# Expert gates of a two-block transformer layer: fp32r one-hot products of 256 columns, four tokens behind each of 64 score blocks

## What is computed

```
q = (xf @ wq).reshape(t, 8, 256)
v1, i1 = top_k(q[..., :128] @ keys1.T, 16);  v2, i2 = top_k(q[..., 128:] @ keys2.T, 16)
top_s, pos = top_k(v1[..., :, None] + v2[..., None, :], 16)      # over 16 x 16 candidates
expert = (i1 * 128 + i2)[pos]                                     # 8 x 16 = 128 picks a token
gate = softmax(top_s)
z = einsum('cd,ced->ce', x, u[expert]);  act = gelu(z) * gate
y = einsum('ce,ced->cd', act, v[expert])
```

## Time and profile before

| what | us |
|---|---|
| median of 3 runs (2815.0 to 2817.1) | 2816.63 |
| the profiled execution | 2815.1 |
| span of the profiled execution | 2813.3 |
| TensorE busy | 2759.1 (98%) |
| VectorE busy | 1811.2 (64%) |
| ScalarE busy | 1391.6 (49%) |
| GpSimd busy | 257.1 (9%) |

### The profile page before, as it was taken

The page is one execution under the profiler, slowest core; times in us unless marked ns, Lnnn a source line. Parts: engine busy times, 40 slices in busy tenths (PEclk is TensorE's granted clock), DMA queues, the critical chain, the costliest instruction groups (busy, mean ns, idle before and its releaser), DMA issues.

```text
span 2813.3 us, 49430 instructions
## 1 busy us (share of the span) xinstructions
PE 2759.1 (98%) x15452; PEld 2411.5 (86%) x15452; DVE 1811.2 (64%) x2894; ACT 1391.6 (49%) x2020; POOL 257.1 (9%) x342
## 2 busy tenths in 40 slices
PE   8999999899999999999999999999999999999998
PEld 6888877788888888889999999888888888888887
DVE  6666655657986666578886666666665555555555
ACT  5454545545565444455555554545554444444444
POOL 0000000000000000000004998000000000000000
PEclk9999999999999999999999999999999999999999
DMA  6544454464554444555565444666665556555574
GB/s 244 191 151 164 162 175 155 165 210 154 167 172 163 157 150 142 186 193 185 183 207 175 159 155 157 216 211 212 209 211 193 194 194 193 191 192 193 193 236 159
DMA packets 153551, 514.71 MB, mean 183 GB/s; under 512 B 17056, under 2 KB 33696, under 8 KB 152480
## 3 DMA queue, kind: packets, MB, share of 16 engines
q1 hardware_dynamic: 131904, 480.44, 52.0%
q10 hardware_dynamic: 21600, 33.70, 3.3%
HBM read 501.49 MB, written 12.58 MB: 183 GB/s over the span
## 4 chain that ended last, share of the span: by engine, by line
PE 59%; DVE 0%; ACT 0%; issue 0%; POOL 0%; DVEq 0%; ACTq 0%; POOLq 0%
PE bank L493 13%; PE bank L2111 8%; PE bank L2113 8%; PE bank L2112 8%; PE bank L498 6%; PE bank L478 3%; PE bank L479 3%; PE bank L480 3%; PE bank L2086 2%; PE bank L533 1%; PE bank L532 1%; PE bank L531 1%; PE bank L2061 0%; DVE act L1086 0%; PE bank L2131 0%
## 5 line engine op out<-in xcount | busy, mean ns | idle before, releaser
L455 DVE TENSOR_TENSOR w_lo<-raw,w_hi 128x1024 fp32r<-128x1024 f32 x904 | 1097.8, 1225 | 816.3 <-ACT w_hi L446 808.9
L446 ACT ACTIVATE w_hi<-raw 128x1024 fp32r<-128x1024 f32 x904 | 953.2, 1059 | 1027.5 <-PE bank L2113 369.3
L493 PE MATMUL bank<-act,w_hi 128*128 128x512 f32 x3072 | 787.9, 398 | 2.7 <-ACT w_hi L446 1.3
L493 PEld LDWEIGHTS bank<-act,w_hi 128*128 128x128 f32 x3072 | 554.1, 189 | 109.3 <-issue 6.2
L498 PEld LDWEIGHTS bank<-act,w_lo 128*128 128x128 f32 x3072 | 419.1, 190 | 31.2
L498 PE MATMUL bank<-act,w_lo 128*128 128x256 f32 x3072 | 428.1, 282 | 0.0
L2111 PE MATMUL bank<-w_hi,expert_act 128*128 128x512 f32 x1008 | 392.3, 389 | 0.1
L2112 PE MATMUL bank<-w_lo,expert_act 128*128 128x512 f32 x1008 | 392.2, 389 | 0.0
L2113 PE MATMUL bank<-w_hi,expert_act 128*128 128x512 f32 x1008 | 392.1, 389 | 0.0
L478 PE MATMUL bank<-act,w_hi 128*128 128x256 f32 x912 | 261.0, 286 | 3.3 <-DVE w_lo L455 2.7
L479 PE MATMUL bank<-act,w_hi 128*128 128x256 f32 x912 | 258.7, 284 | 0.0
(11 more groups left out here) (286 smaller groups left out, 2380.2 us busy)
## 6 DMA issues: line engine op xcount, KB each, us to landing
raw<-in_stream SPq DMA_DIRECT2D x904, 512.0 KB, 4.2
big<-in_ukv ACTq DMA_DIRECT2D x16, 512.0 KB, 5.2
z_kept<-cst ACTq DMA_DIRECT2D x64, 128.0 KB, 3.2
cst<-z_kept ACTq DMA_DIRECT2D x64, 128.0 KB, 3.9
big<-in_x SPq DMA_DIRECT2D x2, 1024.0 KB, 9.6
big<-in_rows ACTq DMA_DIRECT2D x2, 1024.0 KB, 8.8
big<-in_rg_w ACTq DMA_DIRECT2D x1, 2048.0 KB, 8.2
x_kept<-big ACTq DMA_DIRECT2D x1, 2048.0 KB, 6.6
```

Of the source, the lines that this page charges most:

```text
L446: act.activation(w_hi[:, s, :], raw[:, s, :], ACT.Copy).then_inc(hi_ready, 1)
L455: dve.tensor_tensor(w_lo[:, s, :], raw[:, s, :], w_hi[:, s, :].bitcast(F32), ALU.subtract).then_inc(lo_ready, 1)
L493: pe.matmul(bank[:, :], w_hi[:, s, kk * P:(kk + 1) * P], act2[:, k, :, :].rearrange("p a n -> p (a n)"), start=(k == 0), stop=False)
```

## The change

- `EARLY` becomes 96 and a new `LATE` is 32. `u_gates` now holds 64 score blocks, `u_late` 32. `z_kept` has 96 rows.
- Behind each score block of `u_gates`, after both units, come four tokens in place of eight split over the two units. Each engine's loop has 32 turns of two blocks.
- The gates are split once into `gate_hi` (fp32r, ScalarE) and `gate_lo` (the rest, VectorE). For one token, VectorE writes `weighted[:, s, :, :]`, 256 wide: the one-hot of the first index times the high gates, and beside it the same times the low gates, in one `scalar_tensor_tensor`. GpSimd's one-hot `hot[:, s, :]` is unchanged but for its type.
- The product of a token is one fp32r product with 256 columns. Two tokens fill a bank; a block uses two banks, `banks[0]`, `banks[1]` for even and `banks[4]`, `banks[5]` for odd blocks.
- ScalarE copies the low halves of a bank to `G` (two tokens, 256 values a partition), VectorE adds the high halves to `G` (`add_gates`).
- 64 of the 96 kept blocks are read back and multiplied in the first 32 turns of the stage `v` in place of `u_late`.

The other buffers only move (`hot`, `weighted`, `slot_t` and the parameters' tile `par`, which now also holds the second indices). The diff, cut to its core:

```diff
-         ("wqu", 4 * PH), ("u_decode", 2 * PH), ("u_gates", S // 8), ("u_late", NB // 2), ("v", NB)]
-EARLY = NB // 2
+         ("wqu", 4 * PH), ("u_decode", 2 * PH), ("u_gates", S // 4), ("u_late", NB // 4), ("v", NB)]
+EARLY = 3 * NB // 4
+LATE = NB - EARLY
...
# ScalarE, gate stage
+            act.activation(gate_hi.bitcast(F32R), gate_lo, ACT.Copy).then_inc(slots_kept, 1)
+
+            with act.Fori(0, S // 8) as i:
                 for n in range(2):
-                    def keep_gates(m):
-                        act.wait_ge(hot_used[3], i * 4 + 2 * n + m + 2)
-                        act.activation(G[:, :, bass.ds(i * 16 + (8 * n + 4 * m), 4)],
-                                       banks[m][:, :].rearrange("p (t b) -> p b t", t=4), ACT.Copy)\
-                           .then_inc(gate_kept[m], 1)
-                    ahead(split_hi, act, "u_gates", i, 2, n, units=(0,))
-                    keep_gates(0)
-                    ahead(split_hi, act, "u_gates", i, 2, n, units=(1,))
+                    for u in range(2):
+                        ahead(split_hi, act, "u_gates", i, 2, n, units=(u,))
                     act.wait_ge(unit_done, 2 * pair_of("u_gates", i, 2, n) + 2)
                     act.wait_ge(z_saved[n], i * 16 + (32 * PH + 1))
                     low_half(act, GZ[:, n, :], banks[2 + n])
-                    keep_gates(1)
+                    for half in range(2):
+                        act.wait_ge(hot_used[2 * half + 1], i * 2 + n + 2)
+                        act.activation(G[:, :, bass.ds(i * 8 + (4 * n + 2 * half), 2)],
+                                       GATE_BANKS[n][half].rearrange("p (t a b) -> p a b t", t=2, a=2)[:, 1, :, :],
+                                       ACT.Copy).then_inc(gate_low, 1)
                     wait_summed(act, block_of("u_gates", i, 2, n))
                     act.activation(GZ[:, n, :], GZ[:, n, :], ACT.Gelu).then_inc(gelu_ready[n], 1)
                     act.wait_ge(gelu_ready[n], i + (2 * PH + 2))
...
# ScalarE, stage v, first 32 turns
+            with act.Fori(0, (EARLY - LATE) // 2) as i:
+                for n in range(2):
+                    act.wait_ge(early_ready[n], i + (LATE // 2 + 1))
+                    act.dma_start(GB[:, n, :], z_kept[bass.ds(i * 2 + (LATE + n), 1), :, :]
+                                  .rearrange("o p n -> (o p) n")).then_inc(z_back[n], 16)
+                next_experts(i)
...
# VectorE, gate stage
+            def add_gates(i, n):
+                for half in range(2):
+                    dve.wait_ge(gate_low, i * 4 + (2 * n + half + 1))
+                    dest = G[:, :, bass.ds(i * 8 + (4 * n + 2 * half), 2)]
+                    high = GATE_BANKS[n][half].rearrange("p (t a b) -> p a b t", t=2, a=2)[:, 0, :, :]
+                    dve.tensor_tensor(dest, dest, high, ALU.add).then_inc(gate_kept[n], 1)
+
+            with dve.Fori(0, S // 8) as i:
                 for n in range(2):
-                    for s in range(8):
-                        tok = i * 16 + (8 * n + s)
-                        dve.wait_ge(hot_used[s % 4], i * 4 + (2 * n + s // 4) + 1)
-                        dve.tensor_scalar(hot[:, 0, s % 4, :], iota, slot_t[:, 0, bass.ds(tok, 1)],
-                                          slot_t[:, 2, bass.ds(tok, 1)], ALU.is_equal, ALU.mult).then_inc(hot1, 1)
-                        if s % 4 == 3:
-                            ahead(split_lo, dve, "u_gates", i, 2, n, units=(s // 4,))
+                    for s in range(4):
+                        tok = i * 8 + (4 * n + s)
+                        dve.wait_ge(hot_used[s], i * 2 + n + 1)
+                        dve.scalar_tensor_tensor(
+                            out=weighted[:, s, :, :], in0=iota.unsqueeze(1).broadcast_to([P, 2, P]),
+                            scalar=first_index[:, bass.ds(tok, 1)],
+                            in1=slot_t[:, 1:3, bass.ds(tok, 1)].broadcast_to([P, 2, P]),
+                            op0=ALU.is_equal, op1=ALU.mult).then_inc(hot1, 1)
+                        if s == 1 and n == 1:
+                            add_gates(i, 0)
+                        if s % 2:
+                            ahead(split_lo, dve, "u_gates", i, 2, n, units=(s // 2,))
                     add_halves(dve, GZ[:, n, :], banks[2 + n], block_of("u_gates", i, 2, n))
+                add_gates(i, 1)
...
# VectorE, stage v, first 32 turns
+                    next_expert(i, n)
+                    dve.wait_ge(z_back[n], i * 16 + (8 * LATE + 16))
+                    back = G[:, bass.ds(i * 2 + (LATE + n), 1), :].rearrange("p o n -> p (o n)")
+                    dve.tensor_tensor(back, GB[:, n, :], back, ALU.mult).then_inc(early_ready[n], 1)
...
# TensorE, gate stage
+            with pe.Fori(0, S // 8) as i:
                 for n in range(2):
                     pe.wait_ge(gelu_ready[n], i + (2 * PH + 1))
-                    for m in range(2):
-                        halves_out(pe, pair_of("u_gates", i, 2, n), n, banks[2 + n], units=(m,))
-                        pe.wait_ge(gate_kept[m], i * 2 + n + 1)
-                        for s in range(4):
-                            pe.wait_ge(hot1, i * 16 + (8 * n + 4 * m + s + 1))
-                            pe.wait_ge(hot2, i * 16 + (8 * n + 4 * m + s + 1) + 1)
-                            pe.matmul(banks[m][:, s * P:(s + 1) * P], hot[:, 1, s, :], hot[:, 0, s, :], start=True,
-                                      stop=True).then_inc(hot_used[s], 1)
+                    halves_out(pe, pair_of("u_gates", i, 2, n), n, banks[2 + n])
+                    pe.wait_ge(gate_kept[n], i * 2 + 1)
+                    for s in range(4):
+                        pe.wait_ge(hot1, i * 8 + (4 * n + s + 1))
+                        pe.wait_ge(hot2, i * 8 + (4 * n + s + 1) + 1)
+                        pe.matmul(GATE_BANKS[n][s // 2][:, (s % 2) * S:(s % 2 + 1) * S], hot[:, s, :],
+                                  weighted[:, s, :, :].rearrange("p a b -> p (a b)"), start=True, stop=True)\
+                          .then_inc(hot_used[s], 1)
```

More of the change, by code:

```diff
@@ L83 @@
 _n = 0
-for _name, _count in [("conv", 4 * CONV_J), ("rnn", 2 * KT), ("heads", 2 * H2), ("u_gates", S // 8),
-                      ("u_late", NB // 2)]:
+for _name, _count in [("conv", 4 * CONV_J), ("rnn", 2 * KT), ("heads", 2 * H2), ("u_gates", S // 4),
+                      ("u_late", LATE)]:
     HALVED[_name] = _n
@@ L157, in build @@
             pass
-        hot = sb("hot", [P, 2, 4, P])
+        weighted = sb("weighted", [P, 4, 2, P], F32R)
+        with nc.sbuf_tensor("below_hot", [P, CONST["causal"][0]], F32), \
+                nc.sbuf_tensor("hot", [P, 4, P], F32R) as hot:
+            pass
         cst = sb("cst", [P, CONST_W])
@@ L260, in build @@
         G = big[:, :].rearrange("p (b t) -> p b t", b=NB)
+        first_index = slot_t[:, 0, :]
+        second_index = par[:, 0:S]
+        gate_hi = slot_t[:, 1, :]
+        gate_lo = slot_t[:, 2, :]
+        GATE_BANKS = [[banks[0], banks[1]], [banks[4], banks[5]]]
         GZ = c("band").rearrange("p (s n) -> p s n", s=2)
@@ L615, in _ @@
                     pool.sem_inc(hot_turn, 1)
-                    pool.tensor_scalar(hot[:, 1, s % 4, :], iota, idx8[:, s:s + 1], None, ALU.is_equal)\
+                    pool.tensor_scalar(hot[:, s % 4, :], iota, idx8[:, s:s + 1], None, ALU.is_equal)\
                         .then_inc(hot2, 1)
@@ L1010, in expert_hi @@
                 act.activation(expert_hi_t[:, n, :], G[:, bass.ds(b, 1), :].rearrange("p o n -> p (o n)"), ACT.Copy)                   .then_inc(eh_ready, 1)
-            with act.Fori(0, EARLY // 2 - 1) as i:
+            with act.Fori(0, LATE // 2 - 1) as i:
                 late_turn(i)
@@ L1016, in _ @@
                 expert_hi(n, n, 2 * FIRST["u_late"])
-            late_turn(EARLY // 2 - 1)
+            late_turn(LATE // 2 - 1)
             for n in range(2):
-                act.wait_ge(act_ready[n], EARLY // 2 + 1)
-                act.wait_ge(early_ready[n], EARLY // 2 + 1)
+                act.wait_ge(act_ready[n], LATE // 2 + 1)
+                act.wait_ge(early_ready[n], LATE // 2 + 1)
             def next_experts(i):
@@ L1024, in next_experts @@
                     expert_hi(i * 2 + (2 + n), n, 2 * pair_of("v", i, 2, n) + 2)
-            with act.Fori(0, NB // 2 - 8) as i:
+            with act.Fori(0, (EARLY - LATE) // 2) as i:
[4 more added lines that the diff above has]
+                next_experts(i)
+            for n in range(2):
+                act.wait_ge(early_ready[n], EARLY // 2 + 1)
+            with act.Fori((EARLY - LATE) // 2, NB // 2 - 8) as i:
                 next_experts(i)
@@ L1682, in _ @@
                 ahead(split_lo, dve, "u_decode", 0, 2, _)
-            dve.wait_ge(slots_kept, 3)
-            with dve.Fori(0, S // 16) as i:
-                for n in range(2):
-                    for s in range(8):
-                        tok = i * 16 + (8 * n + s)
```

(44 more changed lines are left out.)

9 lines of the change are left out of this document (4 added, 5 removed).

## The result

The changed kernel takes 2830.89 us (median of 5 runs, 2830.15 to 2831.41), the kernel before 2816.28: the ratio is 1.0056, with a 95% interval of 1.0044 to 1.0067. It is 14.6 us slower. The forecast was 8.5 us slower, with a range of 2806 to 2836, in which 2830.9 lies. The profiled execution has a span of 2828.2 us, 14.9 more than before.

The account below looks back on a forecast made before the run. TensorE, busy 98%, was taken to wait on a chain through ScalarE and VectorE: 32 x 13.43 + 0.6 = 430.4, plus 178.8 for late scores, 609.2 us against 600.7, 8.5 us slower: 2823.6 us, range 2806 to 2836.

Parts of the forecast that it names:

- narrow bounds: Whole kernel: 2820 to 2832 us, the forecast case with the wide one-hot priced cheaper or dearer.
- price of the wide one-hot: VectorE, gate stage: 0.48 us long, 0.40 apart; bounds 0.34 apart, 3.5 us off, and 0.52 to 0.60, 7.7 more.
- What bounds, and the products: Gate stage: TensorE bounds; four products take 0.47 us in place of 0.93, a block 6.06 if nothing waits.
- rival A: Gate stage: faster, the chain does not reach TensorE, 6.06 us a block, 2781.6 us in all; chance 0.15.
- The chain: Gate stage: TensorE waits for tokens 2 and 3's one-hots behind VectorE's split, through ScalarE's DMA issue; 13.43 us per two blocks.
- The term that was too small: Chain's end, from ScalarE's high split to TensorE's next scores: 3.49 us, including 0.11 more for a product that waited.
- binding term: ScalarE's next split at 9.94 us after an odd block, with its loop jump, plus 3.49: 13.43 us per two blocks.
- The start: Gate stage's first block: tokens 2 and 3 come late, about 7.3 us, 0.6 more than the mean.
- B: Gate stage: about the same, only the short chain binds, 6.48 us a block, 2808.5 us in all; chance 0.15.
- C: Gate stage: slower, GpSimd governs, held up by wide one-hots, 7.0 us a block, 2842 us in all; chance 0.08.
- D: Gate stage: VectorE blocks behind GpSimd at unit 1's low split, 10 to 19 us more, about 2838; chance 0.05.
- What the profile was to show: Gate stage: two unequal blocks 13.4 us apart, and about 120 TensorE idle times or long weight loads, released by wide one-hots.

Follow-up runs that it names:

- e1: Changed kernel with VectorE writing the wide one-hots of all four tokens ahead of unit 0's low split: 2783.17 us, 0.989 of the kernel before.
- e2: Changed kernel with the wide one-hots of tokens 0, 1 and 2 ahead of unit 0's low split, only token 3 behind it: 2818.52 us.
- e3: Changed kernel with ScalarE issuing the DMA of the even block's gelu after the odd block's unit 0 high split, not before: 2829.18 us.
- e7: Kernel before with the fp32r products, split gates, wide one-hots, two-token banks and adds, still eight tokens behind each of 32 blocks: 2846.43 us, ratio 1.0114.
- e8: Changed kernel with TensorE's and ScalarE's gate-stage loops over four blocks a turn in place of two: 2825.84 us.
- e5: Changed kernel with fp32 products of 128 columns, 128-wide one-hots, no split of the gates and one ScalarE copy of four tokens: 2822.91 us.

## Why the prediction was right, and where it was short

**The range.** That the narrow bounds, 2820 to 2832, held is in part luck. They allowed for another price of the wide one-hot, and that price came out as forecast; what was missing lay in a term without bounds, below.

**What bounds, and the products.** Right. Four fp32r products take 0.48 us where they follow each other (e1: 1702.04 to 1702.52); the forecast had 0.47. TensorE alone would run at 6.07 a block, forecast 6.06, and e1 reached that: 2783.2, where rival A had 2781.6 for the case that the chain does not reach TensorE.

**The chain.** Right as a mechanism and nearly in every link. The forecast's steps were 1.17, 1.15, 0.44, 0.59, 0.47, 1.18, 1.15, and 0.40 + 0.48 for the two wide one-hots; the trace of after has 1.18, 1.15, 0.45, 0.58, 0.47, 1.18, 1.15 and 0.87. e1 and e2 show that these one-hots behind that split are the cause, and their number the dose. The lines in question, ns min/median/max:

```profile
L1718 DVE SCALAR_TENSOR_TENSOR weighted<-cst,slot_t x256: 469/479/594, 1510.9 to 1943.6; 128x256 fp32r<-128x256 f32 x128
...
L465 DVE TENSOR_TENSOR w_lo<-raw,w_hi x122: 1224/1226/1227, 1518.8 to 1931.1; 128x1024 fp32r<-128x1024 f32 x122
...
L626 POOL TENSOR_SCALAR hot<-cst,stat x256: 593/602/1664, 1510.5 to 1939.9; 128x128 fp32r<-128x128 f32 x128
```

The wide one-hot is 0.48 us, as taken from line 1431.

**The term that was too small** is the last one, "a product that had to wait takes 0.34 to the next start in place of 0.23 ... together 3.49", which was the same for every block. It was mis-sized where TensorE's loop jumps. From the last product to the next scores it is 0.22 us inside a turn (about 1705.48 to 1705.70), but 0.64 (1712.10 to 1712.74; 0.60 in the median) where the turn ends: a jump that is hidden when instructions are queued ahead shows when TensorE has just waited, and I had counted such a jump for ScalarE and not for TensorE. The other two misses are small: TensorE wakes 0.13 us after the one-hot, not 0.05, and the even block has unit 1 done at 5.88 after its start, not 5.79, since its first high product takes 0.33 us to the next in place of 0.24. So the pair measured above is 9.61 + 3.49 + 0.41 + 0.08 + 0.09 = 13.68. Here 9.61 + 3.49 = 13.10 is the forecast's own chain after an even block. Its binding term, 13.43 by ScalarE's jump after an odd block, was not the longest; there ScalarE had 0.95 us from DMA issue to split and waited for TensorE.

Over 32 pairs, 13.65 against 13.43 is 7.0 us. The start took 1.0 us beyond 32 pairs, forecast 0.6, and a timeline shows that first block:

```profile
1512.97 0.98 DVE L1718 SCALAR_TENSOR_TENSOR weighted<-cst,slot_t 128x256 fp32r<-128x256 f32 x2
...
1513.69 0.38 PE L2128 MATMUL bank<-weighted,hot 128*128 128x256 f32 x1 [0.64 <-DVE weighted L1718]
...
1514.40 0.39 PE L2128 MATMUL bank<-weighted,hot 128*128 128x256 f32 x1 [0.33 <-POOL hot L626]
```

The third product waited 0.64 us for its wide one-hot, the fourth 0.33 for GpSimd. The two misses, 7.4 us, less what the stage before gave (0.6) and 0.4 in the expert stage, are the 6.4 us by which the span's increase exceeds the forecast.

**The rivals.** A became true only in e1. B (short chain alone, 2808.5, 12.96 a pair) was mispriced mostly by the same missing term: e3, where it binds, has 13.58 a pair and 2829.2. C did not come: GpSimd waits for TensorE for most of its idle time, its median one-hot is 0.602 us, and the products waited for it three times, 1.7 us in all. It does come in part in e7, where GpSimd's median rises to 0.846 and weight loads wait for its one-hots 38 times between 1560 and 1740 us, 11.5 us in all. D did not come. In 122 low splits of the changed kernel the longest is 1.227 us, 0.001 over the median, while one-hots on GpSimd were stretched to 1.664. In e7, where both engines are nearly full, the longest split is 0.14 over the median and a one-hot reaches 1.962. The rule of the Trainium skill, "SBUF — State Buffer", section "SBUF: two separate sides", that whichever of the two starts first makes the other wait, is thus seen in one direction here; in the other the most that appears is 0.14 us, not a one-hot's 0.60. In 64 cases of the changed kernel a one-hot had begun 0.24 us or more before the split and was still running; in 62 of them both kept their usual length, and by the median the split began 1.18 us after ScalarE's, as it does without a one-hot in its way.

**What the profile was to show.** Unequal blocks, 7.00 and 6.64, came as said. The idle times did not come as said: the waits view puts nearly all of them down to "issue" and to ScalarE's `w_hi`, not to the wide one-hot. The row at 1712.74 names ScalarE's split, which that product does not wait for; its end merely fell nearby. The timeline, not the releaser, showed the cause.

## What to carry to other kernels

Free time on every engine is no proof that a shorter period fits: follow one turn through all queues, and put work that waits for nothing new ahead of work that waits. When TensorE waits for a small operand, look at what stands before it in the producer's queue; here a reordering of a few lines on VectorE turned a loss of 0.6% into a gain of 1.1%. And price each loop jump that comes right behind a wait. A small edit is read from the length of its stage, not from the total, when an unchanged stage ahead of it varies by as much.

## What was not expected of the hardware

A loop jump on TensorE costs nothing visible while products are queued (e1: blocks of 6.07 us throughout, with a jump after every second), and 0.36 to 0.41 us right behind a waiting product. A second effect looked like a part of the jump and is not: in even blocks after waiting products the first eight high products last 2.10 us, not 2.00, in e8 also where no jump stands before them (the row at 1711.98). In e5, with fp32 products, the odd blocks show it too. What causes it stays open.
